# A two-block network on one core: the order of weight splits, residual sums and one transpose is changed

## What is computed

```python
# first block: gated recurrence and mixer, then a gated feed-forward network with a 3x3 convolution
x = x + mx2 * merge_branches(...)              # w_a, w_b, w_out
x = x + mx5 * conv_ffn(h2, ffn_up, ..., ffn_down)
x = rmsnorm(x, final_g)
# second block
x = x + hybrid_mixer(rms_norm(x), ...)         # ends with "@ w_out", here called w_out2
h = rms_norm(x, norm_xattn_w); m = rms_norm(mem, norm_mem_w)
q = (h @ wq).reshape(b, s, 4, 256)             # four heads
k, v = split(m @ wkv)                          # wk and wv
probs = softmax(q @ k.T * 256 ** -0.5)
x = x + (probs @ v).reshape(b, s, 1024) @ wo
h = rms_norm(x, norm_ffn_w)
u = conv3(h @ w_up)                            # 2 * 2816 columns, here up2
x = x + (silu(u[:, :2816]) * u[:, 2816:]) @ w_down   # down2
return rms_norm(x, norm_final_w)
```

## Time and profile before

| | us |
|---|---|
| median of 3 runs | 909.63 (908.51 to 910.71) |
| profiled execution, its own time | 910.43 |
| its span in the trace | 908.6 |
| TensorE matmul busy | 864.0 (95%) |
| VectorE busy | 583.0 (64%) |
| ScalarE busy | 459.4 (51%) |
| GpSimd busy | 441.8 (49%) |

### The profile page before, as it was taken

How to read it: one execution, slowest core, us unless ns; L and a number is a source line. 1 busy time by engine, 2 the same in 40 slices (tenths; PEclk the granted TensorE clock), 3 DMA queues, 4 the chain that set the end, 5 groups by cost and what they waited for, 6 DMA issues and landing times.

```text
span 908.6 us, 16200 instructions
## 1 busy us (share of the span) xinstructions
PE 864.0 (95%) x6564; PEld 822.1 (90%) x6564; DVE 583.0 (64%) x1188; ACT 459.4 (51%) x745; POOL 441.8 (49%) x217
## 2 busy tenths in 40 slices
PE   6799999998899999999999899899999999999995
PEld 2388999997699999999999899899999999999994
DVE  6988987874566697677675659676558433333435
ACT  5332344442556565555554755455446554555553
POOL 0756412322472588888888200000003688888781
PEclk9899999999899999999999999899999999999997
DMA  9857565654275366655566445254535465565641
GB/s 344 337 202 253 185 235 155 222 160 165 93 230 190 126 193 199 183 182 185 186 184 187 131 139 186 71 162 121 182 95 161 128 212 176 182 188 183 186 139 48
DMA packets 45759, 160.96 MB, mean 177 GB/s; under 512 B 5218, under 2 KB 5490, under 8 KB 45556
## 3 DMA queue, kind: packets, MB, share of 16 engines
q1 hardware_dynamic: 45680, 159.91, 54.7%
q10 hardware_dynamic: 4, 0.01, 0.0%
HBM read 158.85 MB, written 1.05 MB: 176 GB/s over the span
## 4 chain that ended last, share of the span: by engine, by line
PE 77%; DVE 12%; ACT 4%; issue 3%; DMA 2%; POOL 1%; SPq 0%; DVEq 0%; ACTq 0%
PE bank L625 16%; PE bank L621 16%; PE bank L623 16%; PE bank L929 4%; PE bank L927 4%; PE bank L925 4%; DVE wlo L490 3%; ACT whi L1112 2%; PE bank L730 2%; PE bank L814 1%; DMA ada_kT<-in_adaT 1%; PE bank L690 1%; PE bank L643 1%; PE bank L647 1%; PE bank L671 1%
## 5 line engine op out<-in xcount | busy, mean ns | idle before, releaser
L490 POOL TENSOR_TENSOR wlo<-raw,whi 128x1024 fp32r<-128x1024 f32 (+1 forms) x177 | 411.8, 2347 | 391.8 <-ACT whi L1112 391.7
L1112 ACT ACTIVATE whi<-raw 128x1024 fp32r<-128x1024 f32 (+1 forms) x253 | 258.3, 1026 | 80.7 <-PE bank L625 41.5
L625 PE MATMUL bank<-h2l,whi 128*128 128x256 f32 x848 | 240.9, 284 | 2.5 <-DVE h2l L1510 2.4
L621 PE MATMUL bank<-h2h,whi 128*128 128x256 f32 x848 | 242.2, 286 | 0.5 <-ACT h2h L1336 0.5
L623 PE MATMUL bank<-h2h,wlo 128*128 128x256 f32 x848 | 240.4, 284 | 0.0
L1510 DVE SCALAR_TENSOR_TENSOR accs<-bank,vec,accs 128x189 f32<-128x189 f32 (+4 forms) x440 | 161.1, 433 | 72.3 <-ACT accs L1382 72.3
L625 PEld LDWEIGHTS bank<-h2l,whi 128*128 128x128 f32 x848 | 163.2, 192 | 3.5 <-DVE h2l L1510 3.5
L621 PEld LDWEIGHTS bank<-h2h,whi 128*128 128x128 f32 x848 | 163.3, 193 | 1.4 <-ACT h2h L1336 0.7
L623 PEld LDWEIGHTS bank<-h2h,wlo 128*128 128x128 f32 x848 | 163.3, 193 | 0.1
L490 DVE TENSOR_TENSOR wlo<-raw,whi 128x1024 fp32r<-128x1024 f32 x76 | 92.3, 1223 | 26.9 <-ACT whi L1112 26.4
L929 PE MATMUL bank<-gl,whi 128*128 128x256 f32 x352 | 99.7, 283 | 1.3 <-DVE gl L1507 1.3
(11 more groups left out here) (316 smaller groups left out, 1670.3 us busy)
## 6 DMA issues: line engine op xcount, KB each, us to landing
raw<-in_up SPq DMA_DIRECT2D x88, 512.0 KB, 3.6
raw<-in_w_in SPq DMA_DIRECT2D x45, 512.0 KB, 3.7
raw<-in_down SPq DMA_DIRECT2D x44, 512.0 KB, 3.8
ada_kT<-in_adaT SPq DMA_DIRECT2D x22, 512.0 KB, 4.3
raw<-in_w_out SPq DMA_DIRECT2D x16, 512.0 KB, 4.0
raw<-in_w_in_t SPq DMA_DIRECT2D x12, 512.0 KB, 4.5
ada_vM<-in_adaT SPq DMA_DIRECT2D x10, 512.0 KB, 4.7
ada_buf<-in_adaT SPq DMA_DIRECT2D x8, 512.0 KB, 10.9
```

Source lines behind the costliest of these rows:

```text
L490: return e.tensor_tensor(wlo[:, j % HL, 0:k], raw[:, j % RAW, 0:k], whi[:, j % HL, 0:k].bitcast(F32), ALU.subtract)
L621: e.matmul(ps, wh[:, k, :], xh(k), start=k == 0, stop=False)
L625: t = e.matmul(ps, wh[:, k, :], xl(k), start=False, stop=k == KTILES[name] - 1)
L1112: e.activation(whi[:, j % HL, 0:(k1 - k0) * 128], raw[:, j % RAW, 0:(k1 - k0) * 128], ACT.Copy).then_inc(S.hi.up(j))
```

## The change

There are three edits.

1. In the residual loops of `w_out2` and `wo`, ScalarE splits the weights first (j < 7), then waits for the new x and makes `h2h` and the squares; at j = 7 `sqrt_next()` comes before `h2h` instead of behind it. VectorE makes the low halves behind the residual sum and the addition of squares, where they stood ahead of the wait for the chunk; only `los` up to the fourth chunk stays ahead of step 0.
2. The low halves of three chunks, `up2` 0, 22 and 1, the first three of `up2` in the list, go from GpSimd to VectorE.
3. For the last head TensorE issues `turn(3)` between the two halves of `mem_value(3)`, and ScalarE makes `PT` after one split, ahead of the second split and of `vM`.

```diff
--- before.py
+++ after.py
@@ -139,7 +139,9 @@
 
     out = []
     for j, (name, n, _, _) in enumerate(CHUNKS):
-        if name in ("up", "down", "up2", "down2") or (name == "wk" and n in (4, 5)) or (name == "wv" and n < 2):
+        if name == "up2" and n in (0, 1, NFF):
+            out.append("dve")
+        elif name in ("up", "down", "up2", "down2") or (name == "wk" and n in (4, 5)) or (name == "wv" and n < 2):
             out.append("pool")
         elif j <= ch("w_in", IN_Q + 3):
             out.append("pool")
@@ -648,7 +650,8 @@
                         if k == KT - 1:
                             t.then_inc(S.chunk.up(c))
 
-            def lin_tok(name, n, outs, x, frees):
+            def lin_tok(name, n, outs, x, frees, between=None):
+
 
                 xh, xl, high, high_event, low, low_event = x
                 for half in range(2):
@@ -671,6 +674,8 @@
                             t = e.matmul(ps, xl(k)[:, sl], wh[:, k4, :], start=False, stop=k == KT - 1,
                                          skip_group_check=True)
                     t.then_inc(S.chunk.up(c))
+                    if between and half == 0:
+                        between()
 
             def means(key, src, n, signal, event, until, by=0):
 
@@ -889,9 +894,9 @@
                 slot, free = lin_ring.take(("wk", j), S.kT, j)
                 lin("wk", j, banks[slot][:, 0:L], mn, free, beside)
 
-            def mem_value(n):
+            def mem_value(n, between=None):
                 slot, free = lin_ring.take(("wv", n), S.vM, (n, 1))
-                lin_tok("wv", n, [banks[slot]], mn, [free])
+                lin_tok("wv", n, [banks[slot]], mn, [free], between)
 
             residual("w_out", merged, 2)
             mem_key(0)
@@ -1081,8 +1086,7 @@
                 if h:
                     scores(h)
                     mix(h - 1)
-            mem_value(3)
-            turn(3)
+            mem_value(3, lambda: turn(3))
             mix(3)
             residual("wo", of("oh", "ol", S.oh, lambda k: k // 2, S.ol, lambda k: k // 2))
 
@@ -1328,6 +1332,11 @@
                 if name not in ("down", "down2"):
                     splits(ch(name, 0) + HL)
                 for j in range(8):
+                    if name in ("w_out2", "wo"):
+                        if j < 7:
+                            splits(ch(name, j) + HL + 1)
+                        else:
+                            sqrt_next()
                     if name in AHEAD:
                         if j == 0:
                             w.wait_ge(S.chunk, H2_READ[name])
@@ -1339,9 +1348,7 @@
                         if j == 3:
                             splits(ch("wv", 0) + HL)
                     else:
-                        if j < 7 and name != "down2":
-                            splits(ch(name, j + 1) + HL)
-                        if j == 7:
+                        if j == 7 and name == "down2":
                             sqrt_next()
                         squares(name, j, xT[:, j, :])
                 if name == "down":
@@ -1484,8 +1491,9 @@
                 t.then_inc(S.soft.up(h))
                 if h:
                     mix(h - 1)
+            splits(ch("wv", 6) + HL)
+            turn(3)
             mem_value(3)
-            turn(3)
             mix(3)
             residual("wo")
             ffn(1, "up2", "down2")
@@ -1869,7 +1877,8 @@
                         w.wait_ge(*((S.summed, (f, j | 1)) if j < 6 else (S.chunk, ch(name, NFF - 1))))
                     else:
                         ps = lin_bank((name, j))[:, 0:L]
-                        los(ch(name, j) + HL)
+                        if j == 0:
+                            los(ch(name, 0) + HL)
                         w.wait_ge(S.chunk, ch(name, j))
                     if name == "down":
                         t = stt(xT[:, j, :], ps, mod[:, 40 + j, 0:1], xT[:, j, :], ALU.mult, ALU.add)
@@ -1887,6 +1896,8 @@
                         if j:
                             add_squares(name, j - 1)
                         if name in AHEAD:
+                            if j < 7:
+                                los(ch(name, j) + HL + 1)
                             low(j)
                 if name == "down":
                     low(6)
```

## The result

| | before | after |
|---|---|---|
| median, us | 909.63 (908.51 to 910.71) | 904.91 (901.83 to 905.71) |
| profiled execution, us | 910.43 | 905.71 |
| its span, us | 908.6 | 903.9 |

What follows compares the result with a forecast made beforehand. TensorE was taken to bound the kernel (77% of the span), with time won only at its holes and half clock. -1.2 - 2.1 - 1.4 + 0.1 = -4.6 us gave 905.1 us for the median, range 903.8 to 907.6.

Steps and rivals of the forecast that it cites:

- The pace of the loop: In the `w_out2` loop VectorE sets 3.09 us a step against TensorE's 2.88, because the split comes after `h2h`.
- Leaving `w_out2`, -1.2 us: At the passage from `w_out2` to `wq` the holes close: -1.2 us, with bounds 0.9 to 1.35.
- The 0.49 us before the squares and the 0.68 before `h2h`: Leaving `w_out2`: the savings expected from TensorE's waits before the sum of squares and for `h2h` 7.
- the wait before the spread: Leaving `w_out2`: a further wait on TensorE, whose disappearance was counted only in the upper bound of 1.35 us.
- Leaving `wo`, -2.1 us: At the exit of `wo`, without GpSimd's three low halves VectorE's stretched instructions shorten and the hole goes: 1.87 to 2.2 us.
- The table load in its new place: Step 7 of `wo`: loading the Sqrt table ahead of `h2h` 7 costs 0.1 us at most, so nothing.
- The clock, -1.4 us: Behind `wo`, 707.1 to 710.4 us: the half clock follows TensorE's idling and goes with the hole, saving 1.14 to 1.65 us.
- The last turned probabilities, +0.1 us: Before the last mix, the hole is moved from `PT` to `vM`, not removed: +0.1 us (-0.1 to +0.25).
- Hidden low halves on VectorE: Steps 4 to 6 of `wo`: three added low halves of 1.22 us make 2.54 us a step, hidden by TensorE's 2.88.
- the rival that `up2` eats the gain: In `up2`, low halves and splits hold TensorE and the saved time is lost: -1.1 us, 908.5 us; chance 0.05.
- The rival on the other side: Last `wo` steps: long VectorE instructions are slow in themselves and three low halves add waiting: +2.6, 912.2 us; chance 0.04.

Runs made afterwards that it cites:

- e4: The changed kernel with VectorE's old order in the residual loops, ScalarE's new order kept: median 903.67 us, ratio 0.9943 to the kernel before.
- e5: The changed kernel with ScalarE's old order in the loops, including the old table-load place, VectorE's new order kept: 917.44 us, ratio 1.0099 to before.
- e9: The kernel before with three `up2` low halves on VectorE and `sqrt_next()` ahead of the last `h2h`: median 906.43 us, ratio 0.9983.
- e10: The kernel before with only `sqrt_next()` moved ahead of the last `h2h` in both loops: median 907.5 us, ratio 0.9992.
- e6: The kernel before with the low halves of `wq` 0 to 3 on GpSimd instead of VectorE: median 913.73 us, ratio 1.0063.
- e3: The kernel before with the second edit alone, low halves of `up2` 0, 22 and 1 on VectorE: median 909.16 us, ratio 0.9995.
- e2: The kernel before with the first edit alone, both new loop orders, those `up2` low halves still on GpSimd: median 904.96 us, ratio 0.995.
- e1: The kernel before with the third edit alone, `turn(3)` inside `mem_value(3)` and `PT` ahead of `vM`: median 910.64 us, ratio 1.0009.
- e8: The changed kernel with `mix(2)` moved on TensorE between `mem_value(3)` and `mix(3)`: median 903.03 us, ratio 0.9938 to the kernel before.

## Why the prediction was right, and where its reasons were not

**The pace of the loop: right.** "ScalarE makes `h2h`, only then the split" was the cause of 3.09 us a step. e4 and e5 part the two halves: with ScalarE's new order 2.88 us, with VectorE's new order alone 3.48. What the prediction didn't say is that VectorE's half of the edit is useless.

**Leaving `w_out2`, -1.2 us: under-sized.** Columns (a) and (b) give 1.26 + 0.33 = 1.59, above my upper bound of 1.35. The 0.49 us before the squares and the 0.68 before `h2h` were right to 0.1; missing was most of the second 0.33. I had given the wait before the spread 0.15 us, at the upper bound alone. From the sum of squares to the spread it was 0.21 (1.73 to 1.52), and 0.12 behind the spread; about 0.10 of the whole comes with the place of the table load alone (column b of e9 and e10, 6.86).

**Leaving `wo`, -2.1 us: the size right (2.17), the reason half wrong.** The step that failed is "I read this as VectorE standing still while GpSimd works on SBUF. The last `h2l` is late by that", with the whole hole put down to it. GpSimd does stretch these instructions (e6), but putting the three low halves on VectorE alone gives nothing (e3), and the new order without it gives 1.50 of the 2.17 us (e2). The hole had two causes beside each other, the stretched addition and the table load, on top of VectorE's lag. Low halves moved alone leave column (d) at 5.15, the load moved alone at 5.15, both 3.81, and the new order in addition 3.00. The paragraph on the table load asked only what it costs in its new place ("so nothing") and not what it had cost in the old one. The chain of waits names the one that came last; that the other lay 0.2 us off could have been read from the earlier trace rows and one row more: the addition started at 702.21 ends at 704.61, the tiny Sqrt starts at 703.89, and the squares behind it end at 704.40.

```profile
704.00 0.40 ACT L1135 ACTIVATE sq<-xT 128x256 f32<-128x256 f32 x1
```

**The table load in its new place: right,** no cost at all. From the load's start to the next instruction it is 1.30 us (698.40 to 699.70), against 1.29 in the kernel before. The 2.66 us of the Trainium skill, "ScalarE: Activation LUTs", section "What ACT_TABLE_LOAD costs", are not borne out in these rows: by them, an estimate, `h2h` 7 would have started about 1.4 us later.

**The clock, -1.4 us: right in this trace (1.45), and the rule behind it too simple.** I tied the fall to the hole. No trace without a hole at `wo`'s exit shows a fall there, but e6 has one of 1.97 us there, and e10 two of 1.30 and 0.68 us, and neither shows a fall. The busy time and clock of e6, first behind `w_out2`'s exit, then behind `wo`'s:

```profile
623.60:630.00 6.40, 6.37 (x30) 6.40 (x31) 1.72 (x3) 2.87 (x4) 0.00 (x0) 0.50 0.30 84
707.00:717.00 10.00, 8.26 (x68) 7.89 (x67) 4.73 (x8) 6.50 (x12) 6.92 (x3) 1.00 0.49 141
```

Behind the 4.27 us hole the clock is at 0.50, 1.2 GHz, and behind the one of 1.97 us at 708 it stays at 1.00. What the fall of 3.4 us costs can be read without a model: column (f) is 21.06 to 21.14 with it (before, e1, e3) and 19.54 to 19.62 in all kernels without, 1.5 us. (In e5 the fall begins at 711.7 and so lies in part in columns d and e.) What decides at a hole of about 2 us stays open. These are single traces: e6's own executions have a mean granted clock of 0.977, as the traced one, in three cases and of 0.975 in three, so a kernel may not do the same each time.

**The last turned probabilities, +0.1 us: right,** 0.00 measured in e1. "The hole is moved, not removed" is what the rows show.

**Hidden low halves on VectorE: right.** Three more at 1.23 us cost nothing. And time saved ahead of `up2` reached the end in every kernel: 166.92 us from the first to the last `down2` product throughout, so the rival that `up2` eats the gain is out. The rival on the other side, that the long instructions are slow in themselves, is out by e6 and e3.

**The number: near in part by luck.** The traces give 5.10 us where the sum has 4.6: `w_out2` gave 0.4 us more. The traced execution of the changed kernel reached `w_out2` 0.39 us later than that of the kernel before, its five executions lie between 901.83 and 905.71 us, and the kernel before has two groups of times 3.8 us apart. That the median of 904.91 lies 0.2 us from the forecast says less than the table does. (The working itself gives 909.63 - 4.6 = 905.03, not 905.1.)

## What to carry to other kernels

When two engines feed each other in a loop, put on each first what waits only for the pacing engine, and behind it what waits for the other: here the split ahead of `h2h` took 0.21 us from each step, while VectorE's new order with ScalarE's old one made the kernel 7.5 us slower. The gains of parts need not add up: ScalarE's and VectorE's new order together brought 4.55 us by the table (e2), the low halves and the place of the load without the rest 2.92 us (e9), and all of it 5.10. A hole can have two chains of nearly equal length behind it; before pricing a fix, follow the second one too, and try the parts alone and together. To move a wait to another place of the same chain won nothing here (e1); independent matmuls put into the hole won 1.02 us (e8).

## What was not expected of the hardware

- A low half on GpSimd (2.4 us) stretches VectorE instructions with two SBUF inputs to 2.3 to 2.6 us and leaves one with a PSUM input at 0.41 us; two VectorE instructions in a row can each wait for one of GpSimd's (e6: 2.38 and 2.56 us), which made a hole of 4.27 us.
- A hole of 1.85 to 1.99 us on TensorE was followed by half the clock in three traces (before, e1, e3) and by full clock in one (e6 at 708 us); two holes of 1.30 and 0.68 us (e10) were followed by full clock.
- The same kernel ran with a mean granted clock of 0.977 in some executions and of 0.981 in others, 3.8 us apart.
- The first `w_out2` matmul started between 591.2 and 595.6 us in the twelve profiled executions, though the program ahead of it was the same.
